# A tile of 32 bytes in front of the residual stream, in a kernel that runs two transformer blocks on one core

## The reference

```python
h = x
for i in range(2):                       # first block: i = 0 NSA, i = 1 SSD
    m = mixer_i(rms_norm(h, gains[i, 0]))
    h = h + rms_norm(m, gains[i, 1])
    f = conv_ffn(rms_norm(h, gains[i, 2]))      # (h @ w_up), conv of 3, silu(gate) * val, @ w_down
    h = h + rms_norm(f, gains[i, 3])
u = rms_norm(h, norm_pre_mix)            # second block: GDN and memory attention
h = h + rms_norm(concat(gdn(u), mem_attention(u, mem)) @ w_out, norm_post_mix)
f = (silu(g) * u2) @ w_ffn_out           # g, u2 = split(rms_norm(h, norm_pre_ffn) @ w_ffn_in)
return h + rms_norm(f, norm_post_ffn)
```

## The kernel before

| tile | first byte | rest | use |
|---|---|---|---|
| `raw` x3, `whi` x4, `wlo` x4 | 16512, 41088, 73856 and on by 8192 | 0 | weights |
| `masks` | 110144 | 64 | the identity of all transposes among them |
| `grow` | 116640 | 32 | a gain row |
| `nhalf` | 120736 | 32 | one number |
| `h` | 120768 | 64 | residual stream |
| `xT` x2 | 128960, 137152 | 64 | rows, turned, high and low |
| `xs`, `grow2` | 149504, 153600 | 0 | scratch, a gain row |
| `gT`, `yT`, `yG` (each laid over the same place) | 157696 | 0 | what the down-projections hold |
| `mT` x2 | 202752, 210944 | 0 | the memory's rows, turned |
| `X` x2 | 191104, 195232 | 0, 32 | windows for the compression, held from many offsets |
| `pj`, `Ct`, `LY`, `TU`, `vb` | from 182880 | 32 or 96 | the delta rule |

## Time and profile before

### The profile page before, as it was taken

One profiled execution on the slowest core, in us unless ns is written; L12 is line 12 of the kernel. 1 busy time (PEld: TensorE's weight loads), 2 busy tenths in 40 slices (PEclk: granted clock), 3 DMA queues, 4 the chain that ended last, 5 costly groups with the idle time before them and its releaser, 6 DMA issues.

```text
span 1202.5 us, 23183 instructions
## 1 busy us (share of the span) xinstructions
PE 1176.9 (98%) x9852; PEld 1076.7 (90%) x9852; DVE 847.2 (70%) x1299; ACT 651.3 (54%) x1171; POOL 151.4 (13%) x143
## 2 busy tenths in 40 slices
PE   8999999999999999999999999999999999999998
PEld 8897789999889898978999988999989878999986
DVE  6677777888557988886788874857577776655542
ACT  4657556666446665644666653665435534644431
POOL 1320000000002332101000000103443311000000
PEclk9999999999999999999999999999999999999999
DMA  8842225565625443353755564442222322755540
GB/s 308 268 141 89 98 101 207 192 210 194 231 106 176 151 182 141 114 184 105 259 196 181 206 245 158 178 176 106 107 107 71 120 93 92 277 196 190 184 167 35
DMA packets 31622, 196.67 MB, mean 164 GB/s; under 512 B 4000, under 2 KB 5664, under 8 KB 9376
## 3 DMA queue, kind: packets, MB, share of 16 engines
q1 hardware_dynamic: 27504, 185.17, 43.1%
q10 hardware_dynamic: 4016, 10.03, 2.6%
HBM read 193.09 MB, written 1.05 MB: 161 GB/s over the span
## 4 chain that ended last, share of the span: by engine, by line
PE 88%; DVE 5%; ACT 3%; issue 2%; POOL 1%; DMA 0%; DVEq 0%; POOLq 0%; ACTq 0%
PE bank L538 24%; PE bank L540 24%; PE bank L539 24%; DVE wlo L527 2%; PE bank L1894 1%; PE bank L1132 1%; PE bank L1189 1%; PE bank L1216 1%; ACT whi L519 1%; PE bank L725 1%; PE bank L2538 1%; PE bank L3005 1%; PE bank L2481 1%; POOL rr L667 0%; PE bank L2525 0%
## 5 line engine op out<-in xcount | busy, mean ns | idle before, releaser
L527 DVE TENSOR_TENSOR wlo<-raw,whi 128x1024 fp32r<-128x1024 f32 x322 | 389.0, 1245 | 87.9 <-ACT whi L519 87.3
L538 PE MATMUL bank<-xT,wlo 128*128 128x256 f32 x1488 | 418.6, 281 | 4.2 <-DVE wlo L527 2.1
L539 PE MATMUL bank<-xT,whi 128*128 128x256 f32 x1488 | 413.1, 278 | 0.0
L540 PE MATMUL bank<-xT,whi 128*128 128x256 f32 x1488 | 413.1, 278 | 0.0
L519 ACT ACTIVATE whi<-raw 128x1024 fp32r<-128x1024 f32 (+1 forms) x349 | 349.2, 1048 | 115.9 <-PE bank L540 86.7
L538 PEld LDWEIGHTS bank<-xT,wlo 128*128 128x128 f32 x1488 | 279.5, 188 | 7.9 <-DVE xc L1601 2.8
L539 PEld LDWEIGHTS bank<-xT,whi 128*128 128x128 f32 x1488 | 279.6, 188 | 0.6 <-issue 0.5
L540 PEld LDWEIGHTS bank<-xT,whi 128*128 128x128 f32 x1488 | 279.4, 188 | 0.0
L667 POOL TENSOR_TENSOR rr<-rr,nhalf 128x1 f32<-128x1 f32 x34 | 24.7, 729 | 710.0 <-DVE rr L655 522.4
L538 PE MATMUL bank<-whi,gT 128*128 128x512 f32 x264 | 104.6, 396 | 0.0
L540 PE MATMUL bank<-whi,gT 128*128 128x512 f32 x264 | 104.4, 395 | 0.0
(11 more groups left out here) (390 smaller groups left out, 1766.5 us busy)
## 6 DMA issues: line engine op xcount, KB each, us to landing
raw<-in_wall SPq DMA_DIRECT2D x173, 1024.0 KB, 4.8
grow<-in_rows ACTq DMA_DIRECT2D x13, 512.0 KB, 5.3
h<-in_x SPq DMA_DIRECT2D x4, 256.0 KB, 5.3
dsk<-in_rows ACTq DMA_DIRECT2D x4, 256.0 KB, 3.4
memx<-in_mem ACTq DMA_DIRECT2D x1, 1024.0 KB, 10.5
out<-h SPq DMA_DIRECT2D x4, 256.0 KB, 2.0
masks<-in_masks SPq DMA_DIRECT2D x1, 580.0 KB, 13.3
D<-Tx ACTq DMA_DIRECT2D x4, 128.0 KB, 5.8
```

What stands on the lines that cost most here:

```text
L527: e.tensor_tensor(low, src, high, SUB).then_inc(*up("dve.low", p))
L538: e.matmul(out, a[1], b[0], start=start, stop=False)
L539: e.matmul(out, a[0], b[1], start=False, stop=False)
L540: return e.matmul(out, a[0], b[0], start=False, stop=stop)
```

## The change

One tile of 128 x 8 float32, 32 bytes in each partition, is made between `nhalf` and `h`. Nothing reads or writes it. All tiles made after it (`h`, `xT`, `ss`, `rr`, `sqj`, `xs`, `grow2` and all that is laid out for single stages) begin 32 bytes later: `xT` at 128992 and 137184, `gT` at 157728, `mT` at 202784. All tiles made before it, the weights' buffers, `masks` and `grow` among them, stay. Every queue holds the same instructions in the same order, with the same shapes and waits.

```diff
         grow = sb([128, 1024], name="grow")
         nhalf = sb([128, 1], name="nhalf")
+        sb([128, 8], name="space")
         h = sb([128, 2, 1024], name="h")
         xT = [sb([128, 8, 256], f32r, name="xT") for _ in range(2)]
         ss = sb([128, 8], name="ss")
```

## The result

With the unused 32 bytes the kernel takes 1227.68 us (median of 4, 1227.23 to 1228.48), before 1207.52 us. The ratio is 1.0178, 95% interval 1.0154 to 1.0202: slower by 20 us. The profiled execution took 1227.81 us with a span of 1226.0 us, 23.5 us more than the span of before.

The account below looks back on a forecast made before the run. The prediction took TensorE's pace of fp32r matmuls as the bound. Its terms, 12.3 + 0 + 1.9 + 0 = 14.2 us, on the median of 1207.5 gave 1221.7 us, likeliest 1222, range 1197 to 1238.

Parts of the forecast that it names:

- the likeliest case: Fast streams moving `xT` past held weights slow to 117.8 ns or so: 1215 to 1226 us, chance 0.34.
- `xT` at `mT`'s pace: All matmuls moving `xT` at 120 ns: 22.1 us more, 1231.5 us; chance 0.14 shared with an extra piece.
- an extra piece: Each moving operand touches 17 pieces of 64 bytes, not 16: 7.2 ns each, 1231 to 1240 us; chance 0.14, shared.
- The bound: Whole kernel: the pace of fp32r matmuls on TensorE sets the end; effects on VectorE, ScalarE or DMAs are mostly hidden.
- First kind: `xT` moving past held weights: 2736 matmuls in the three nets lose 4.5 ns each, 12.3 us; the other 1728 lose 0.
- Rests by 128: Start addresses modulo 128: weights and `mT` at 0, `xT` going from 64 to 96, half way to `mT`'s place.
- Second kind: Weights moving past held `xT`, 3 x 288 matmuls: 1.9 us if all take the slow pace; bounds -1.9 and +6.2 us.
- Third and fourth: 512 columns of weights past held `gT`, `yT` or `yG`; then other engines, transposes and DMAs: 0 us each.
- the prediction's other sum: Moving `xT` at 120 ns everywhere, 22.1 us, plus 1.9 us for held `xT`: 1231.5 us.
- Nothing changes: Rival for the whole kernel: a 32-byte shift keeps each operand's place in its 16-byte line; 1204 to 1211 us, chance 0.24.
- The faster rival: Slow moving and held uses of `xT` all reach 113.3 ns: 9.7 us less, 1197.8 us; range 1196 to 1203, chance 0.28.
- A pace redrawn in each execution: Condition for the prediction being wrong: matmul pace varies by execution and has nothing to do with the tile; no size given.

Follow-up runs that it names:

- TensorE alone: Kernels computing no layers, only matmul streams with other engines idle; at the addresses of the kernel before, rows 32 bytes later: 120.0 ns, unshifted 113.3 or 117.8.
- the two kernels at other distances: Two matmul-only kernels, high and low tiles 8320 bytes apart, not 8192, and tiles at other distances than the kernel before; first 115.5 to 120.0 ns, second mostly 117.6 to 118.0.

## Why the prediction came out as it did

The time is inside the range and on the forecast side; 14.2 us were forecast and 20.2 measured. It is outside the likeliest case, 1215 to 1226 us, and lies in the one that was given 0.14, `xT` at `mT`'s pace or an extra piece. By the prediction's own steps:

- **The bound.** Right. The span grew by 23.5 us and TensorE's busy time by 24.5, while VectorE and ScalarE stayed as they were. They only wait longer, as the lists of waits have it (us in total, times, longest), before and then after:

```profile
DVE wlo L527 <- ACT whi L519: 87.3, 77, 4.9
ACT whi L519 <- PE bank L540: 86.7, 35, 3.7
...
ACT whi L520 <- PE bank L541: 104.0, 39, 3.7
DVE wlo L528 <- ACT whi L520: 101.0, 80, 4.6
```

- **First kind, moving `xT`.** The mechanism, where the rows stand against the held weights, was right; the term was too small. I took the middle pace, 117.8 ns; it is 120.0, that of `mT` before. The 2736 of the three nets lose 6.7 ns each and not 4.5: 18.3 us for 12.3. The other 1728 were put at 0 and lose 2.2 ns each, 3.8 us. The prediction had this sum as 22.1 us, and judged it less likely. The middle pace was taken as the nearest to the best that had been seen; no row showed this distance.
- **Rests by 128.** The prediction says that `mT` begins at the same rest as the weights. By 128 it does; by 256, the period that was found, it stands 128 bytes from them. `xT` did move half way towards `mT`'s place, as it says, but its pace became `mT`'s and not one between.
- **Second kind, held `xT`.** 1.9 us forecast, 2.5 measured (115.4 to 118.3 ns).
- **Third and fourth.** 0 forecast. Held `gT` went from 233.2 to 233.4 ns from start to start, VectorE's operation stayed at 473. The zero for `gT` was luck more than cover: other distances change it from 233 to 229 and 227 ns, so the 233 ns do not hide this effect.
- **The base.** The sum was made against the median of 1207.5, of an execution whose span of 1202.5 us had all three long streams fast. By the heaps of the later runs of before, 1207.5 is a run with one of them slow. From 1204.2 the step is 23.5 us, as by the spans. So the prediction's other sum, 22.1 + 1.9 us, would have hit from the right base: 1228.2 us, where it said 1231.5; and the 14.2 us were further off than 20.2 makes them look.
- **The rivals.** Nothing changes, as I drew it from the 16-byte lines in the Trainium skill ("SBUF — State Buffer", "Door 1: The DMA port swizzle"): refuted, since the shift of `xT` by two such lines makes the whole difference. Starts 8 bytes off a multiple of 16 are slower on average, 120.2 against 117.9 ns, so such lines may still play a part. The extra piece of 64 bytes: refuted by the kernel with everything shifted. The faster rival, that the slow streams are freed: wrong for 32 bytes. With 128 bytes seven of the 13 short streams of 48 matmuls are at 113.3 ns in the profiled execution, where before one was, but one long stream is slow there, and the whole kernel's gain is about that of held `gT`, `yT` and `yG`, 6.6 us.
- **A pace redrawn in each execution** was named as what would make it wrong. It exists before, but in the kernel after every stream of the profiled execution is at 120.0 ns, and its four runs lie within 1.3 us.
- **The chances.** Those of the four cases add up to 1.00, and all four lie in or within 2 us of 1197 to 1238, so no case stands behind the 0.2 that was left outside.

What is shown: the cause is the place of `xT` against the weights (`xT` alone moved gives all of it, all moved gives none), it needs no other engine (TensorE alone gives 120.0 against 113.3 or 117.8), and the pace of moving rows as a function of the shift repeats after 256 bytes. That TensorE's reads of its two operands get in each other's way is the likely reading of this, but only argued. What stays open is why the curve has the shape it has, what in a stream's beginning makes it take one pace or the other, how tiles that TensorE doesn't read in these streams change the odds, and whether the place of the high tile against the low one counts as well, which the two kernels at other distances suggest and no run separates.

## What to carry to other kernels

Where TensorE is the bound and streams fp32r, two builds that differ in one small tile can differ by 2%, so look at the remainder of a division by 256 of the distance between what moves and what is held before believing in a gain from an unrelated edit. Read the pace from the starts in the timeline, in several places, for the same instruction; two or three sharp values and a run time in steps (here 4.1 us) mean that streams have taken different paces, and not noise. Take more than three runs of each, since a median of few can be a matter of which heap they fell into. A few unused bytes, tried at several sizes, are a cheap knob: 32 cost 1.8% here, 128 gained 0.5%.

## What the hardware showed that was not expected

- The pace of a matmul of 256 fp32r columns at the full granted clock depends on the distance of its operands, between 113.3 and 122.3 ns, and repeats after 256 bytes.
- At some distances a stream takes one of two or three exact paces when it starts and keeps it for 912 matmuls and through four buffers of weights. One small matmul more ahead of it is enough to change it (113.3 with 4, 117.8 with 5, 113.3 with 6, at the same addresses).
- Matmuls of 512 columns feel it too: 233, 229 or 227 ns, and 234 with only the weights moved.
- Tiles that a stream neither reads nor writes can change how often it takes the slow pace: 32 bytes behind `xT` put six of ten runs near 1216 us, where before 14 of 19 were near 1204.
